# Splitting each 512-column matmul of a kernel's last stage into two of 256 columns with the same stationary operand

## The reference

```python
def chunk(args):
    xt, et, gt = args
    u = expert_down[et]
    h = jax.nn.gelu(jnp.einsum('cd,ced->ce', xt, u), approximate=False)
    vv = expert_up[et]
    return jnp.einsum('ce,ced->cd', gt * h, vv)
...
y_p = peer(h, ...)
h = layer_norm(ALPHA * h + y_p, ln2_g[l], ln2_b[l])
```

## Time and profile before

| | |
|---|---|
| median of 3 runs | 2432.38 us (2431.77 to 2435.62) |
| the profiled execution | 2433.66 us |
| its span, first to last instruction | 2431.4 us |
| PE busy | 2404.8 us, 99% |
| mean granted clock of TensorE | 0.998 |

### The profile page before, as it was taken

The page is one execution under the profiler, slowest core; times in us unless marked ns, Lnnn a source line. Parts: engine busy times, 40 slices in busy tenths (PEclk is TensorE's granted clock), DMA queues, the critical chain, the costliest instruction groups (busy, mean ns, idle before and its releaser), DMA issues.

```text
span 2431.4 us, 45146 instructions
## 1 busy us (share of the span) xinstructions
PE 2404.8 (99%) x15884; PEld 2207.9 (91%) x15884; DVE 1569.1 (65%) x2615; ACT 1197.4 (49%) x1787; POOL 594.7 (24%) x427
## 2 busy tenths in 40 slices
PE   8999999999999999999999999999999999999997
PEld 8999999999999999999999999999888888888886
DVE  5555555546666666888888887755655555555556
ACT  4444444545444444666555655454444444444444
POOL 0000000000000000477668886786000000000000
PEclk9999999999999999999999999999999999999999
DMA  7667666554445665588888998988776777677764
GB/s 270 217 217 223 220 227 210 179 190 151 157 141 172 192 197 184 192 222 220 227 288 223 255 276 288 281 225 259 241 240 230 240 242 242 232 239 242 243 233 139
DMA packets 182918, 539.01 MB, mean 222 GB/s; under 512 B 53664, under 2 KB 53664, under 8 KB 180432
## 3 DMA queue, kind: packets, MB, share of 16 engines
q1 hardware_dynamic: 124128, 449.89, 56.3%
q0 software_dynamic: 54128, 71.68, 12.0%
q10 hardware_dynamic: 4608, 16.78, 2.2%
HBM read 501.42 MB, written 35.78 MB: 221 GB/s over the span
## 4 chain that ended last, share of the span: by engine, by line
PE 98%; DVE 1%; DMA 1%; ACT 0%; issue 0%; DVEq 0%; ACTq 0%; SPq 0%
PE ps L1256 38%; PE ps L1477 28%; PE ps L1452 17%; PE ps L1453 9%; PE ps L1456 1%; PE ps L1295 1%; PE ps L1310 1%; PE ps L1455 1%; PE ps L1303 0%; PE ps L1297 0%; DMA raw<-stream 0%; PE ps L1430 0%; PE ps L1311 0%; PE ps L1290 0%; DVE u_s L1209 0%; DVE u_s L1219 0%
## 5 line engine op out<-in xcount | busy, mean ns | idle before, releaser
L756 DVE TENSOR_TENSOR w_first<-raw,w_first 128x1024 fp32r<-128x1024 f32 x425 | 521.0, 1226 | 367.0 <-ACT w_first L457 355.9
L390 POOL DMA_INDIRECT g_dram<-lists x256 | 442.7, 1729 | 97.8 <-issue 79.1
L457 ACT ACTIVATE w_first<-raw 128x1024 fp32r<-128x1024 f32 x425 | 447.8, 1054 | 4.2 <-DMA raw<-stream 3.3
L756 DVE TENSOR_TENSOR w_second<-raw,w_second 128x1024 fp32r<-128x1024 f32 x299 | 365.9, 1224 | 5.4 <-ACT w_second L457 5.0
L1452 PE MATMUL ps<-a_all,w_first 128*128 128x480 f32 x1024 | 345.8, 384 | 0.2 <-DVE w_first L756 0.2
L1256 PE MATMUL ps<-a_all,w_first 128*128 128x256 f32 x2520 | 315.0, 281 | 9.2 <-DVE w_first L756 9.2
L457 ACT ACTIVATE w_second<-raw 128x1024 fp32r<-128x1024 f32 x299 | 314.6, 1052 | 7.2 <-DMA raw<-stream 6.3
L1256 PEld LDWEIGHTS ps<-a_all,w_first 128*128 128x128 f32 x2520 | 299.2, 189 | 10.2 <-issue 9.2
L1256 PE MATMUL ps<-a_all,w_second 128*128 128x256 f32 x2520 | 303.9, 276 | 0.0
L1452 PE MATMUL ps<-a_all,w_second 128*128 128x480 f32 x896 | 302.1, 382 | 0.0
L1256 PEld LDWEIGHTS ps<-a_all,w_second 128*128 128x128 f32 x2520 | 294.4, 188 | 0.0
(11 more groups left out here) (230 smaller groups left out, 3410.2 us busy)
## 6 DMA issues: line engine op xcount, KB each, us to landing
raw<-stream SPq DMA_DIRECT2D x850, 512.0 KB
g_dram<-blank POOLq DMA_DIRECT2D x32, 512.0 KB, 6.2
a_dram<-act ACTq DMA_DIRECT2D x32, 512.0 KB
a_in<-a_dram POOLq DMA_DIRECT2D x32, 512.0 KB, 5.0
g_in<-g_dram POOLq DMA_DIRECT2D x32, 512.0 KB, 6.5
g_dram<-lists POOLq DMA_INDIRECT x256
res<-x_t SPq DMA_DIRECT2D x4, 512.0 KB, 7.0
ln_s<-ln POOLq DMA_DIRECT2D x1, 2048.0 KB, 7.4
```

Source lines behind the costliest of these rows:

```text
L390: pool.indirect_dma_start(out=g_cell, out_offset=bass.IndirectOffsetOnAxis(ap=lists[0:n, tt, 1, j, c:c + 1], axis=0), in_=lists[0:n, tt, 2 ...
L457: act.activation(weights(t, hf, moved)[0], raw[:, t.slot(hf), :], ACT.Copy).then_inc(hi_ready, 1)
L756: dve.tensor_tensor(low, raw[:, s, :], high.bitcast(F32), ALU.subtract).then_inc(lo_ready, 1)
```

## The change

Each piece of 512 columns becomes two pieces of 256, one behind the other, with the same stationary operand and in the same bank of PSUM. Over the first tile the flag that starts an accumulation is set on the first piece of each bank only. `up_bank` keeps its 512 columns.

```diff
-                        for c in range(2):
-                            o = D * tt + HALF * hf + 512 * c
-                            ins = pe.matmul(ps[:, o:o + 512], m[:, b % 2, s], w[:, 512 * c:512 * c + 512],
-                                            start=first and q == 0, stop=False, skip_group_check=True)
+                        for c in range(4):
+                            o = D * tt + HALF * hf + 256 * c
+                            ins = pe.matmul(ps[:, o:o + 256], m[:, b % 2, s], w[:, 256 * c:256 * c + 256],
+                                            start=first and q == 0 and c % 2 == 0, stop=False, skip_group_check=True)
```

## The result

The changed kernel takes 2451.31 us, median of 6 runs (2450.58 to 2455.38), against 2432.07 us for the kernel before (6 runs: five from 2431.00 to 2435.62, and one of 7957.65 that nothing on record explains). The ratio is 1.0077, with a 95% interval of 1.0067 to 1.0087. It is slower by 0.8%; I had forecast 2427 us, a gain. The time lies within the range of 2424 to 2456 us, at the price of the rival called the slow rhythm (2453 us), which had 23 in 100.

What follows compares the result with a forecast made beforehand. PE's own matmul pace was taken to bound the kernel. Two 256-column steps (227.2 ns) less one of 512 (229.0 ns), times 3024, gave -5.5 us; 2432.38 - 5.5 = 2426.9, so 2427 us, range 2424 to 2456.

Steps and rivals of the forecast that it cites:

- the slow rhythm: Rival, 23 in 100: 256-column matmuls in `up` run at 117.9 ns, not 113.6, giving +20.6 us, 2453 us.
- What bounds the stage: In `up`, PE's own pace is the bound: 3024 matmuls in 692.57 us, feeders' margins 1.7 and 5.7 us.
- The sum's form: In `up`, the change is 3024 times (two steps of 256 columns less one of 512), -5.5 us.
- The 512 term: In `up`, a 512-column matmul takes 692.57 / 3024 = 229.0 ns, 15.7 ns over its columns.
- The step that failed: For `up`, a 256-column matmul was given the 113.6 ns read elsewhere; two take 227.2 ns, 1.8 ns less than now.
- The upper bound: Slower rows, second attention 117.9 ns and query projection 119.7 ns a step, would give +20.6 or +31.4 us in `up`.
- The long stretches: Unbroken 256-column stretches elsewhere, up to 173 us, run at 113.6 ns; `up`, also long and unbroken, should too.
- No change: Rival, 20 in 100: the rate in `up` is per column, 114.5 ns for 256 columns, 2432 us.
- A fixed price for each matmul: Rival, 12 in 100: each added matmul in `up` costs 2.9 ns, +8.8 us in all, 2441 us.
- The loop's code: Rival, 7 in 100 together with denser loads disturbing the stream: `up`'s longer loop is refetched 14 times, +34 us, 2466 us.

## Why the prediction was wrong

**What bounds the stage** was right. It is one unbroken piece of PE's own pace before and after, no feeder came near, and the 20.0 us of the piece are the time's change but for 1.1 us ahead of it.

**The sum's form** was right: 3024 times (two steps of 256 less one of 512). The 512 term, 229.0 ns, was read from the stage itself.

**The step that failed** is the next one: "I take this value, since it is the same form of instruction pair in the same density and by far the most frequent". 113.6 ns was read where `full` has its operands, moving at 64 and stationary at 128 or 256, and even there it is one pace of two. In `up` the roles are turned, the distance is -64, and the step is 117.8 ns. The term was 227.2 ns for two and is 235.6, which turns -5.5 us into +20.0. The run with the gap of 128 bytes shows that the value itself was not wrong: moved to +64, the same program takes 113.4 ns and 2424 to 2427 us in eight of twelve runs, the time that I forecast. The order of the matmuls, in which `up` differs from `full` too, left the step at 117.8 ns.

**The upper bound**, 5.66 / 48 = 117.9 ns, was the right row, and its rival named the turned roles as what speaks for it. I weighed it by how many matmuls run at each pace. Frequency was no reason: all those at 113.6 lie at the two pairs of places of `full`, and the tiles at 117.9 in the earlier trace rows lie at the same two. (They are also fewer than the "some 8000" of the prediction: `full` has 7344 matmuls of 256 columns.) Better evidence was already in the rows, and I noted it without using it: a 512-column step of 229.0 ns is 1.8 ns more than twice 113.6, although it has half as many loads. A stage that is slower for each column with fewer loads differs from `full` in something that may hold at the other width too.

**The long stretches** as an argument ("'Up' is long and unbroken, which speaks against") fell too. At this distance the whole 712.57 us are slow.

**No change**, by two to one in "down": the rate for each column is not kept when a piece is cut, in any of the four places.

**A fixed price for each matmul** as the whole effect is refuted, since the split costs +20.0, +40.0, -19.7 or +19.9 us by place alone; the two pieces of 686.0 us, with 6048 and 3024 matmuls, show no sign of one. The rule of the Trainium skill that was weighed there (TensorE: Matmul & The Clock Gate, "Back-to-back issue gap") gives 215.8 and 109.2 ns. No kernel here meets it in "up", where the shortest pieces come to 226.8 and 113.4 ns a step.

**The loop's code** stayed near, with 30 packets in q8, though a round has 384 matmuls and 384 loads now. The Trainium skill's figure of 2048 instructions for PE (Runtime: NRT & Kernel Launch, "Instruction fetch mechanics") is in keeping with the 30 packets, and its sentence on taken branches, which gives a window of two pages, is not, unless the window is larger than it says.

What stays open: why the places work as they do, why it turns round with the width, why `full` is fast at +192 and `up` is not, and what picks one of two paces. Not tried: other distances over a whole stage, places that differ at a fixed distance other than +64, other widths, and the order of `full` at +192.

## What to carry to other kernels

A matmul's step that is read in one stage of a kernel need not hold for another whose operands have other roles and places in SBUF: here the same 256 columns took 113.4, 117.8 or 120.0 ns in one stage as 64 bytes moved. Before a width is changed, compare the excess over the columns in both stages, and take a difference as a sign that something besides the width differs. Where a stage is nothing but back-to-back fp32r matmuls, try the places first: 64 bytes gave 0.26% of the kernel here, and in one run of the worst place for 512 columns the kernel lost 0.6%. A change of width and a change of place should be judged together, since the best place for one width was the worst for the other. And where a kernel has two times with nothing between, look at each group and at the stage's own piece; a median over both describes neither.

## What was unexpected of the hardware

The step of a 512-column fp32r matmul in "up" had three values by place alone, 226.8, 229.0 and 233.4 ns, and that of a 256-column one three as well, 113.4, 117.8 and 120.0 ns, at a granted clock of 1.00 and with no wait of PE. One program with fixed places took some 2425 us or some 2452 us by run, and in the traces tiles of one code and one place take 5.46 or 5.66 us. Twice as many matmuls and loads for the same columns, each width at its best place, took 686.07 against 685.96 us.
